# Fused two-block transformer kernel: the order of work between the first output projection and the first expert rows

## The reference, cut to what matters

```
rq, rk, rv, rg, dq, dk, dv = jnp.split(h @ w_in[layer], IN_SPLITS, axis=-1)
ret_lat, ret_ctx = retention_group(rq, rk, rv, rg, crq, crk, crv, crg, ...)
diff_lat, diff_ctx = diff_attention_group(dq, dk, dv, cdq, cdk, cdv, ...)
x = x + mod[:, 2] * (jnp.concatenate([ret_lat, diff_lat], axis=-1) @ w_out[layer])
h2 = modulate(x, norm2_g[layer], mod[:, 3], mod[:, 4])
x = x + mod[:, 5] * peer_ffn(h2, peer_w_query, peer_sub_keys, peer_u, peer_v)

# peer_ffn, for a tile of 128 tokens
q = (hb @ w_query).reshape(t, PEER_HEADS, 2, PEER_HALF)
s = jnp.einsum('thpc,hpnc->thpn', q, sub_keys)
v1, i1 = lax.top_k(s[:, :, 0], PEER_TOPK)
v2, i2 = lax.top_k(s[:, :, 1], PEER_TOPK)
cand = (v1[..., :, None] + v2[..., None, :]).reshape(t, PEER_HEADS, PEER_TOPK * PEER_TOPK)
best, pos = lax.top_k(cand, PEER_TOPK)
experts = jnp.take_along_axis(cand_idx, pos, axis=-1)
gate = jax.nn.softmax(best, axis=-1)
act = jax.nn.gelu(jnp.einsum('thkd,td->thk', expert_u[experts], hb), approximate=False)
return jnp.einsum('thk,thkd->td', gate * act, expert_v[experts])
```

## Time and profile before

| | us |
|---|---|
| median of three executions | 1719.26 |
| lowest, highest | 1718.58, 1721.23 |
| span of the profiled execution | 1719.4 |
| PE busy | 1520.7 |
| DVE busy | 752.0 |
| ACT busy | 502.0 |
| first gather issued by POOL | 253.95 |
| first dot product on DVE | 266.62 |
| last gather issued by POOL | 1212.56 |

### The profile page before, as it was taken

The page is one execution under the profiler, slowest core; times in us unless marked ns, Lnnn a source line. Parts: engine busy times, 40 slices in busy tenths (PEclk is TensorE's granted clock), DMA queues, the critical chain, the costliest instruction groups (busy, mean ns, idle before and its releaser), DMA issues.

```text
span 1719.4 us, 15639 instructions
## 1 busy us (share of the span) xinstructions
PE 1520.7 (88%) x5502; PEld 730.4 (42%) x5502; DVE 752.0 (44%) x1816; ACT 502.0 (29%) x1284; POOL 292.4 (17%) x264
## 2 busy tenths in 40 slices
PE   8999998685489894997999897899999999999998
PEld 5444463462153530333343333443444444455443
DVE  2853178866786566456435436532312100031101
ACT  2412134332433223333443224443412110122210
POOL 0000003434434243223212213321000000000000
PEclk9999999896589896898999998899999999999999
DMA  9736339999999999999999999999876677855774
GB/s 371 257 122 227 140 125 406 403 421 421 421 402 421 421 421 421 399 421 420 415 422 419 422 421 420 413 421 422 347 296 235 259 298 284 306 219 217 289 299 185
DMA packets 94029, 586.83 MB, mean 341 GB/s; under 512 B 6912, under 2 KB 7168, under 8 KB 28288
## 3 DMA queue, kind: packets, MB, share of 16 engines
q1 hardware_dynamic: 56080, 313.19, 46.7%
q0 software_dynamic: 37440, 270.55, 38.1%
q10 hardware_dynamic: 432, 2.10, 0.3%
HBM read 584.76 MB, written 1.05 MB: 341 GB/s over the span
## 4 chain that ended last, share of the span: by engine, by line
PE 71%; DMA 18%; DVE 5%; issue 3%; ACT 2%; POOL 0%; SPq 0%; POOLq 0%; DVEq 0%; ACTq 0%
PE bank L1011 34%; DMA arena<-in_peer_rows,pidx 10%; DMA ring<-in_weights 8%; PE bank L1089 7%; PE bank L701 7%; PE bank L1172 4%; PE bank L779 3%; PE bank L976 2%; DVE arena L2145 2%; PE bank L1018 2%; PE bank L987 2%; PE bank L667 1%; PE bank L756 1%; PE bank L1071 1%; DMA ring<-in_w_mod 1%
## 5 line engine op out<-in xcount | busy, mean ns | idle before, releaser
L1646 POOL DMA_INDIRECT arena<-in_peer_rows,pidx x227 | 257.4, 1134 | 578.2 <-PE bank L1172 531.3
L2145 DVE SCALAR_TENSOR_TENSOR arena<-arena,ring 128x1024 f32<-128x1024 f32 x227 | 273.2, 1223 | 111.9 <-DMA arena<-in_peer_rows,pidx 109.1
L1011 PE MATMUL bank<-ring,arena 128*128 128x512 f32 x736 | 319.4, 593 | 0.0
L1011 PE MATMUL bank<-ring,hT_all 128*128 128x512 f32 x544 | 244.4, 605 | 15.6 <-issue 10.6
L1172 PE MATMUL bank<-arena,keep 128*32 128x512 f32 x908 | 159.8, 704 | 101.1 <-ACT keep L1605 101.1
L1011 PEld LDWEIGHTS bank<-ring,arena 128*128 128x128 f32 x736 | 138.5, 190 | 168.8 <-issue 168.7
L1011 PEld LDWEIGHTS bank<-ring,hT_all 128*128 128x128 f32 x544 | 102.8, 193 | 150.9 <-issue 140.2
L1592 ACT ACTIVATE pf<-pf 128x2 f32<-128x2 f32 x128 | 25.9, 202 | 401.4 <-DVE arena L2145 367.1
L2266 DVE TENSOR_TENSOR x_all<-x_all,bank 128x512 f32<-128x512 f32 x40 | 27.5, 688 | 209.6 <-PE bank L1089 115.8
L1172 PEld LDWEIGHTS bank<-arena,keep 128*32 128x32 f32 x908 | 21.3, 115 | 171.1 <-ACT keep L1605 135.0
L701 PE MATMUL bank<-ring,hT_all 128*128 128x512 f32 x192 | 86.0, 603 | 0.6 <-DVE hT_all L1725 0.6
(11 more groups left out here) (391 smaller groups left out, 1698.2 us busy)
## 6 DMA issues: line engine op xcount, KB each, us to landing
ring<-in_weights SPq DMA_DIRECT2D x122, 2048.0 KB
ring<-in_w_mod SPq DMA_DIRECT2D x12, 2048.0 KB
ring<-in_w_in SPq DMA_DIRECT2D x5, 2048.0 KB
ring<-in_weights SPq DMA_DIRECT2D x8, 1024.0 KB
ring<-in_weights SPq DMA_DIRECT2D x8, 512.0 KB
arena<-in_peer_rows,pidx POOLq DMA_INDIRECT x227
ring<-in_w_in SPq DMA_DIRECT2D x2, 1024.0 KB, 17.6
mem_all<-in_b_mod POOLq DMA_DIRECT2D x3, 512.0 KB, 7.2
```

The lines of the kernel that those rows point to most:

```text
L1011: m = mm(b[:, :], src[:, k], slot8[w][:, k], start=(k == 0), stop=(k == KC - 1))
L1646: nc.gpsimd.indirect_dma_start(out=row_in[n % SLOTS], out_offset=None, in_=a["peer_rows"], in_offset=bass.IndirectOffsetOnAxis(ap=pidx[:, ...
L2145: stt(uslot[n % SLOTS], uslot[n % SLOTS], 1.0, h2g[n % 4], ALU.mult, ALU.mult, accum_out=pact2[:, 16 * (g % 2) + k:16 * (g % 2) + k + 1]). ...
```

## The change

Between the output projection of the first tile and its first gathers, calls are put in another order on PE, ACT and DVE. The same instructions remain, but one matmul of `keep_warm` (L817) is taken away and one small ACT exponential (of `lg`, into an unused column) is added behind the copy of c2x1. The table `UNITS` is changed to match the order on PE. On ACT the last copies before the expert loop (`mix_turn("mr", 1)` and `repeat_copy` of groups 2 and 3) move behind the GELU work of the first two rows. POOL's and SP's lists are as they were.

```
 UNITS
-("A", "q00"), ("D", "p10 p11 k00 p12 p13"),
-("A", "s12a s12b q01"), ("D", "gfirst"), ("A", "s13a s13b"), ("D", "k01 g0"),
+("A", "q00"), ("D", "p10 k00 p11"), ("A", "q01"), ("D", "gfirst p12 p13"),
+("A", "s12a s12b s13a s13b"), ("D", "k01 g0"),
 PE
             h2_turns(0)
-            keep_warm(2)
+            keep_warm(1)
             query("q00", 0, slice(0, P))
             ret_scores(1, 0)
+            key_scores(0, 0)
             ret_scores(1, 1)
-            key_scores(0, 0)
             diff_turn(1, 0)
             mod_rows(10, cpad)
+            diff_turn(1, 1)
             ret_values(1, 0)
-            ret_values(1, 1)
+            query("q01", 1, slice(0, P))
+            regroup_first()
             ret_scores(1, 2)
             ret_scores(1, 3)
-            diff_scores(1, 2)
+            ret_values(1, 1)
             ret_values(1, 2)
             ret_values(1, 3)
-            query("q01", 1, slice(0, P))
-            regroup_first()
+            diff_scores(1, 2)
             diff_scores(1, 3)
-            diff_turn(1, 1)
             diff_values(1, 0)
 ACT
             unit_copy("c2x1", PR[:, 1, 1024:1536], ACT.Silu)
+            f(stat[:, 64:65], lg[:, 0:1], ACT.Exp)
+            h2_turn(0)
             diff_exps(1, 0)
-            h2_turn(0)
             diff_exps(1, 1)
             query_copy("q00")
             diff_copy(1, 0)
+            diff_copy(1, 1)
+            query_copy("q01")
             diff_exps(1, 2)
-            query_copy("q01")
+            diff_exps(1, 3)
             gate_exp(0)
-            diff_copy(1, 1)
             out_squares(2, M[0], (ret_out, 8))
-            diff_exps(1, 3)
             diff_copy(1, 2)
...
             repeat_copy(0, 0)
             repeat_copy(0, 1)
-            mix_turn("mr", 1)
-            repeat_copy(0, 2)
-            repeat_copy(0, 3)
...
-            after = {2: [lambda: gate_exp(1)], ...
+            after = {0: [lambda: mix_turn("mr", 1), lambda: repeat_copy(0, 2), lambda: repeat_copy(0, 3)], 2: [lambda: gate_exp(1)], ...
 DVE
             h2_apply(0)
+            h2_turn(0)
             diff_max(1, 0)
-            h2_turn(0)
             diff_max(1, 1)
             diff_mix(1, 0)
             diff_mix(1, 1)
             decay(1, 0)
-            decay(1, 1)
             key_copy(0, 0)
             half_top(0, 0)
             half_top(0, 1)
             best_pairs(0)
+            rows_of_eight(0)
+            spread_first()
+            decay(1, 1)
+            select_first()
             decay(1, 2)
             decay(1, 3)
-            diff_max(1, 2)
-            rows_of_eight(0)
-            spread_first()
             next_pairs(0)
             on_mod(10)
-            select_first()
+            diff_max(1, 2)
+            diff_max(1, 3)
             diff_mix(1, 2)
-            diff_max(1, 3)
             out_mean(2)
```

2 lines of the change are left out of this document (1 added, 1 removed), and 2 rows, old and new, of the table UNITS.

## The result

The changed kernel took 1725.88 us (median of 20 executions, 1720.9 to 1728.9); the kernel before, on the same chip and in turn with it, 1720.51 us. The ratio is 1.003, with a 95% interval of 1.0022 to 1.0037. By the ratio that is 5.2 us more (the medians are 5.4 us apart), where the forecast had no change. It lies beyond the range's upper end of 1723.6. Of the 2.3 us beyond it, 1.2 us are the kernel before itself, whose median was 1719.26 us when the forecast was made. To a slowdown of more than 3.4 us the prediction gave 0.19. The profiled execution has a span of 1724.0 us against 1719.4. A span is some 1.8 us shorter than the device time of the same execution (1724.0 and 1725.87 here), so a span is compared with a span only.

A forecast was written before the change was run, and what follows sets the result against it. Bound by DMA's bytes until 1200 us, then PE; only bytes delivered by about 300 us count. Terms: -4.6 + 5.7 - 1.0 = +0.1 us, so 1719.4 us; range 1714.8 to 1723.6.

The forecast's parts named there:

- What bounds the kernel: Whole program: DMA from 300 to 1200 us, then PE; the end moves only by bytes DMA delivered by about 300 us.
- First and second chain: Rows 0 to 3: POOL issues row 0 at 249.7 instead of 253.95, row 1 at 253.3 instead of 255.24.
- Third chain: Second tile's attention: last head's transposes 2.6 us later, row 4 issued at 265.1 instead of 262.48, DMA hole of 4.4 us.
- the likeliest case: The forecast itself: clock holds, no change at 1719.4 us, spread -1.0 to +3.2 us; chance 0.50.
- the clock rival: PE's gap before the last head's transposes, 3.9 us, drops the clock to 1.2 GHz: 1723.4 us; chance 0.14.
- Fourth chain: Row 9's wait for PE's first product: ACT's moved copies bring that product 0.7 us earlier despite later dots.
- The drain that the prediction weighed: ACT's GELU table load: a drain of about 1380 ns beside it would make the first product 0.5 us later.
- The sum's last term: DMA at 278 to 286 us: two old dips, 1.0 us together, close through backlog and earlier requests; -1.0 us.
- a lead and two holes: DMA up to 267 us: first bytes 4.6 us earlier, holes of 1.3 and 4.4 us, so 1.1 us behind.
- The rival by which the lead carries through: First row's lead of 4.3 us reaches the end if row 4 isn't late: 1715.0 us; chance 0.20.
- The rival of DVE's delay: DVE stays on the path behind the first rows; 1.3 to 2.6 us reach the end, about 1721; chance 0.12.

The follow-up runs named there:

- e1: The changed kernel with four matmuls of unused result in PE's wait before the last head's transposes; ratio 1.0010 to the kernel before.
- e5: The changed kernel with four unused matmuls in PE's wait before the last head's transposes and four before query q02; ratio 1.0008 to the kernel before.
- e2: The kernel before with three unused matmuls in PE's wait before the last head's transposes; ratio 1.0003.
- g1: The kernel before with the first row's selection put in front, and unused matmuls before the last head's transposes and before q02; ratio 1.0011.
- f3: The kernel before with only q01 and the first row's selection put ahead of the second tile's later work; ratio 1.0010.
- e7: The changed kernel with DVE's out_mean(2) set behind rows_of_eight(1); ratio 1.0020 to the kernel before.
- f1: The changed kernel with DVE's out_mean(2) later and unused matmuls before the last head's transposes and before q02; ratio 0.9991 to the kernel before.
- g3: The kernel before with the selection in front, ACT's last copies behind the GELU, and unused matmuls before the last head's transposes and q02; ratio 0.9992.
- f2: The kernel before with ACT's last copies behind the GELU and unused matmuls before the last head's transposes and before q02; ratio 0.9994.
- e4: The kernel before with only ACT's last copies moved behind the GELU of the first rows; ratio 1.0002.
- e6: The kernel before with ACT's last copies behind the GELU and four unused matmuls before query q02; ratio 0.9988.
- e8: The kernel before with the last head's transposes also made to wait for DVE's spread(0), lengthening PE's gap; ratio 1.0007.
- e3: The changed kernel with ACT's last copies back in front of the first rows' GELU; ratio 1.0037 to the kernel before.
- g2: The kernel before with unused matmuls before the last head's transposes and before q02, nothing else; ratio 1.0009.

## Why the prediction was wrong, step by step

**What bounds the kernel** was right, and so was the rule for the end: it moves by the bytes delivered early (at about 300 us in the prediction, read at 350 here).

**First and second chain** were right: 249.60 against 249.7, and 253.41 against 253.3, the wait for the retention values in front of row 1 included. One slip stands in them: with bytes 1.6 us behind the issue at 249.7 row 0 starts at 251.3 and not at 251.0, so the lead of the first bytes is 4.3 us and not 4.6; the hole behind it is shorter by nearly as much, and the sum hardly moves.

**Third chain.** The count of DVE's new waits was right nearly wait by wait: 1.05, 0.97, 0.88 and 1.24 us for 1.0, 0.8, 1.2 and 1.2. The transposes came at 264.35, 0.65 us behind the 263.7 of the forecast, and within its bounds. Then the chain breaks: PE's gap became 4.29 us, longer than the 3.9 counted, and the clock fell in it. Row 4 came 1.1 us later than forecast, and rows 5 and 6 were held by values that took twice their time: 270.08, where they follow row 4 by 2.0 us in the earlier trace rows's kernel and by 3.84 here.

**The step that failed** is the choice of the likeliest case. The prediction gave 0.50 to a clock that holds through a gap of 3.9 us, and 0.14 to a fall, on two rows of one execution: 3.31 us harmless, 7.10 us not. That was no bound. The gap measured 4.29 us and the granted clock was 0.50 behind it; holding the clock there brings back 3.4 us (e1) and in both gaps 3.8 us (e5) of the 5.2. In e2 and g1 that same wait of 3.31 us was followed by a fall, and in f3 one of 2.80 us was. The rule that spoke against the change was in the text. The Trainium skill, "TensorE: Matmul & The Clock Gate", section "Why this matters for your kernels", tells one to leave no long idle gap between bursts of matmuls; the trace of the changed kernel agrees, with its granted clock of 0.50 behind 4.29 us. The runs give no single length, though: the clock fell behind 2.80 and 2.95 us (f3, e7) and held behind 3.31 in two profiles. One row was too little to set against the rule.

**The price of the clock rival** was about right for its total, and wrong in its parts. 4.0 us over the profiled span were forecast, 3.4 to 3.8 measured (and 5.0 from e7 to f1); the whole loss of 5.2 us is more than this rival had. The first product was to come at 279.5 and came at 277.46, since the clock was back before the second pair of repeats (3.64 us at 274.01). The second fall, at q02, was in no case of mine: I followed the output projection earlier, and didn't ask what PE would meet behind it. The move brings PE to q02 before its weights, and the wait of 2.48 us there (kernel before) becomes 3.66.

**Fourth chain.** With the clock held (e5) the first product comes 50.0 us after ScalarE begins the squares of h2, as it did in the kernel before; 0.7 us earlier was forecast. The last head's transposes come 3.5 us later there by the same count, where 2.65 were forecast. So the mechanism (ACT's copies no longer in front of the GELU) was right, and the attention's extra delay ate the gain. The drain that the prediction weighed doesn't show: the table load takes 1.28 us at 274.03 and the GELU follows it, as in the earlier trace rows.

**The sum's last term**, -1.0 us for old dips that close, failed too. The count up to there (a lead and two holes, 1.1 us behind) is borne out in kind: by 272 us e5, with the clock held, is 0.66 MB or 1.6 us behind. But the sum took DMA's later stretch as able to make 1.0 us good, and from 272 to 350 us e5 moves 31.5 MB and the kernel before 31.6. What is missing at 272 us stays missing, since from row 4 on the rows wait for gates on PE. The rival by which the lead carries through (0.20) had 4.3 us for it and a condition, row 4 not late; in g3 row 4 was issued 0.7 us later than in f2 and the gain was none. Both pairs refute it as priced. A kernel in which every later gate keeps its old place was not run.

**The rival of DVE's delay** (0.12, 1721) is near in size: with the clock held, 1.4 us of loss are left (e5, with an interval that takes in none), and taking an early wait off DVE brings 2.9 (f1). But the rival spoke of DVE's dots and selections behind the first rows; no run shows that they carry the delay.

## What to carry to other kernels

Bringing the first transfer forward gains only as far as the transfer behind the next gate also moves; count the gates behind it before you count the lead. When a reordering lengthens an idle gap on TensorE (here from 2.79 to 4.29 us), take the fall of its clock as the likeliest case unless several executions show a gap as long to be harmless. A few matmuls without use in the gap show what the fall costs; in the kernel that didn't need them their own cost could not be told from nothing (1.0003 and 1.0009). And when one wait is closed, look at what the engine runs into next: what e4 had gained at 272 us was gone 20 us further on, in a wait for weights.

## What was not expected of the hardware

The length of an idle gap on PE did not decide whether the clock fell. In front of the last head it held over 2.78 to 2.79 us in three kernels (before, e4, e6) and fell with 2.80 (f3), 2.95 (e7), 3.45 (e8) and 4.28 to 4.29 (e3 and the change). In front of the first products the wait was 3.31 us in every kernel that had it: the clock held in two profiles (before, g2) and fell in five (e2, g1, e3, e8, f3), in the last three of which it had fallen some 15 us earlier as well. At q02 it held over 2.48 us and fell with 3.45 to 4.17. The clearest pair is e2 and g2. Their instructions are the same up to query q02, the wait is 3.31 us in both, and the first half of the projection behind it takes 8.83 us in one and 7.13 in the other. So neither the gap's length nor what PE did ahead of it decides alone; the two profiles are of different executions on different chips. What decides between 2.8 and 3.3 us stays open.
